# Where VectorE divides a unit of the memory attention: two steps behind its own maximum, instead of behind the next unit's

## The reference, cut to what matters

```python
def mem_attend(h, mk, mv, wq, wo):
    q = jnp.einsum('bsd,dhe->bshe', h, wq)
    s = jnp.einsum('bshe,bmhe->bhsm', q, mk.astype(q.dtype)).astype(jnp.float32) * MEM_SCALE
    pr = jax.nn.softmax(s, axis=-1).astype(q.dtype)
    o = jnp.einsum('bhsm,bmhe->bshe', pr, mv.astype(q.dtype))
    return jnp.einsum('bshe,hed->bsd', o, wo)
```

## Time and profile before

| | |
|---|---|
| median of 3 runs | 2026.81 us (2025.74 to 2030.93) |
| profiled execution | 2026.47 us, span 2024.7 us |
| mean granted TensorE clock | 0.971 |
| busy, share of the span | TensorE 94%, VectorE 49%, ScalarE 35%, GpSimd 5% |

### The profile page before, as it was taken

How to read it: one execution, slowest core, us unless ns; L and a number is a source line. 1 busy time by engine, 2 the same in 40 slices (tenths; PEclk the granted TensorE clock), 3 DMA queues, 4 the chain that set the end, 5 groups by cost and what they waited for, 6 DMA issues and landing times.

```text
span 2024.7 us, 37487 instructions
## 1 busy us (share of the span) xinstructions
PE 1897.0 (94%) x16506; PEld 1733.1 (86%) x16506; DVE 986.5 (49%) x1695; ACT 713.9 (35%) x1272; POOL 94.2 (5%) x100
## 2 busy tenths in 40 slices
PE   6998997999889999999999799989987999999997
PEld 5975775898679999999999478759974999999997
DVE  6676455453335544443367754455432465353533
ACT  4443444552334222221344344353523342121212
POOL 2000000200001000000100000001000100000001
PEclk9998999999999999999999799979999999999998
DMA  5210001453012222222222000014610222222221
GB/s 210 72 39 1 4 2 43 151 167 115 32 46 80 91 88 84 94 84 94 84 74 73 8 3 3 4 54 140 203 44 20 79 79 93 85 85 94 87 91 55
DMA packets 38593, 149.51 MB, mean 74 GB/s; under 512 B 4384, under 2 KB 4544, under 8 KB 36768
## 3 DMA queue, kind: packets, MB, share of 16 engines
q1 hardware_dynamic: 36288, 131.05, 19.6%
q0 software_dynamic: 2144, 16.06, 2.1%
HBM read 139.68 MB, written 7.41 MB: 73 GB/s over the span
## 4 chain that ended last, share of the span: by engine, by line
PE 88%; DVE 7%; ACT 3%; issue 1%; POOL 0%; DMA 0%; DVEq 0%; ACTq 0%; SPq 0%; POOLq 0%
PE PS L514 77%; PE PS L634 8%; PE PS L848 1%; DVE stat L1660 1%; PE PS L942 1%; DVE mP L1669 1%; DVE wL L1351 1%; ACT hH L973 1%; ACT wH L973 1%; POOL sq L450 0%; ACT ell L973 0%; DVE stat L1661 0%; ACT aP L973 0%; ACT sq L973 0%; DMA xT<-x_in 0%
## 5 line engine op out<-in xcount | busy, mean ns | idle before, releaser
L514 PE MATMUL PS<-hH,wH 128*128 128x272 f32 x2272 | 487.9, 297 | 31.3 <-DVE hL L1360 24.2
L514 PE MATMUL PS<-hH,wL 128*128 128x272 f32 x2272 | 476.3, 291 | 0.0
L514 PE MATMUL PS<-hL,wH 128*128 128x272 f32 x2272 | 475.9, 291 | 0.0
L1351 DVE TENSOR_TENSOR wL<-ring,wH 128x1024 fp32r<-128x1024 f32 x238 | 300.9, 1266 | 223.0 <-ACT wH L973 222.6
L514 PEld LDWEIGHTS PS<-hH,wH 128*128 128x128 f32 x2272 | 360.7, 190 | 43.4 <-issue 19.1
L973 ACT ACTIVATE wH<-ring 128x1024 fp32r<-128x1024 f32 x238 | 249.6, 1050 | 334.8 <-PE PS L514 334.8
L514 PEld LDWEIGHTS PS<-hH,wL 128*128 128x128 f32 x2272 | 362.2, 191 | 0.0
L514 PEld LDWEIGHTS PS<-hL,wH 128*128 128x128 f32 x2272 | 360.0, 191 | 0.0
L514 PE MATMUL PS<-hidH,wL 128*128 128x272 f32 x1024 | 212.1, 289 | 0.0
L514 PE MATMUL PS<-hidH,wH 128*128 128x272 f32 x1024 | 211.8, 288 | 0.0
L514 PE MATMUL PS<-hidL,wH 128*128 128x272 f32 x1024 | 211.2, 288 | 0.0
(11 more groups left out here) (279 smaller groups left out, 2476.5 us busy)
## 6 DMA issues: line engine op xcount, KB each, us to landing
ring<-wall SPq DMA_DIRECT2D x238, 512.0 KB, 3.3
lw<-lw_in POOLq DMA_DIRECT2D x2, 2240.0 KB, 9.8
xT<-x_in SPq DMA_DIRECT2D x4, 544.0 KB, 6.7
y_out<-hT SPq DMA_DIRECT2D x8, 272.0 KB, 2.1
mem<-mem_in POOLq DMA_DIRECT2D x2, 1024.0 KB, 5.2
mks<-mks_in POOLq DMA_DIRECT2D x2, 1024.0 KB, 10.1
mvs<-mvs_in POOLq DMA_DIRECT2D x2, 1024.0 KB, 13.4
memk_out<-mkp POOLq DMA_DIRECT2D x2, 1024.0 KB, 6.2
```

The lines of the kernel that those rows point to most:

```text
L514: return e.matmul(out, lhsT=a, rhs=b, start=start, stop=stop)
L1351: tt(wL[:, n % SPLIT], ring[:, n % RING], plain(wH[:, n % SPLIT]), ALU.subtract).then_inc(w_lo, 1)
```

## The change

VectorE's program walks the same list. It still takes the maximum at the score's step. The normalise of a unit no longer stands at the step of its turn but two steps behind its own score, from a table `DIVIDES`. So for all 20 units of both layers VectorE's order becomes normalise of u, then maximum of u + 1. TensorE's and ScalarE's programs are the same.

```diff
 MEM_STEPS += [("turn", len(MUNITS) - 1)] + [("weigh", 4 * MHEADS - 4 + _i) for _i in range(4)]
+
+DIVIDES = {_i + 2: _n for _i, (_kind, _n) in enumerate(MEM_STEPS) if _kind == "score"}
...
                 def attention_mem():
-                    for kind, n in MEM_STEPS:
-                        m = 128 if MUNITS[n][1] < 4 else DEC
+                    for i, (kind, n) in enumerate(MEM_STEPS):
                         if kind == "score":
-                            maximum(n, "m", m, MEM, MEM_SCALE, 4 + n % 2)
-                        elif kind == "turn":
-                            normalise(n, "m", mP, m, MEM)
+                            maximum(n, "m", 128 if MUNITS[n][1] < 4 else DEC, MEM, MEM_SCALE, 4 + n % 2)
+                        if i in DIVIDES:
+                            u = DIVIDES[i]
+                            normalise(u, "m", mP, 128 if MUNITS[u][1] < 4 else DEC, MEM)
                         yield
```

## The result

The changed kernel takes 1998.3 us (median of four runs, 1992.6 to 1999.9) against 2026.9 before, a ratio of 0.985 (95% interval 0.983 to 0.986). The forecast was 1994.3 us, a ratio of 0.984. The profiled execution took 1992.6 us with a span of 1990.8, 33.9 us less than before's span; worked out had been 32.5. It was the fastest of the four: its mean granted clock was 0.970, that of the others 0.964 to 0.967.

The account below looks back on a forecast made before the run. TensorE bounds the kernel, waiting for VectorE's divisions queued behind later maxima. Dense part 11.1 plus tail 5.2 give 16.3 us a layer, 32.5 for two, off the profiled 2026.47: 1994.0, as median 1994.3 us; range 1989 to 2004.

Parts of the forecast that it names:

- The bound: Where memory queries are projected, TensorE waits 32.0 us for the divided tile mP, held in VectorE's queue behind a later maximum.
- The dense part: While the query projection still runs, all waits of units 0 to 12 go: 11.06 us a layer.
- the walk: Step-by-step timing of the new order through the engines by the old trace's durations; 16.3 us a layer saved.
- The cover: Dense part: TensorE's other work hides the divisions, by over 0.8 us behind a query tile's evacuation, 0.3 at a head's end.
- The copy behind the next exponential at a head's end: ScalarE's copy of the turned unit may delay the weighing 0 to 0.3 us, two times a layer; taken as 0.
- The tail: Turns 13 to 19, without dense work beside them, fall from 20.1 to 14.9 us: 5.2 us a layer saved.
- What was to be seen: If right: mP wait falls from 32.0 to 6 to 10 us, all in the tails; a layer's stretch from 91.3 to 75.
- One sign of being wrong: A tail from the last dense step to the weighing of more than 16 us would speak against the forecast.
- Rival 1: Tail gains nothing, since ScalarE's copy may end last there; only units 0 to 13 count, 2001.8 us; chance 0.17.
- rival 3: No change: another wait, for the scores' banks or output copies, ends at the same time; 2026.8 us; chance 0.03.
- rival 4: Slower: VectorE waiting for ScalarE's exponential makes weight-tile splits late; 2030.9 us; chance 0.02.
- Rival 2: TensorE's clock: layer 1's weighing stays at full level, 1992.9 us, or layer 0's falls too, 1995.7; chance 0.08.

Follow-up runs that it names:

- both halves of the order: Two kernels, each giving only some units the change's order, the others as before: units 0 to 13 alone 2002.5 us, units 14 to 19 alone 2015.2 us.
- the pads: Changed kernel plus about 0.8 us idle VectorE work between exponential and reciprocal: units 0 to 12 in one kernel, 14 to 19 in another; 1999.6 and 2004.0 us.
- one-step order: Changed kernel with all divisions one step behind their own maximum instead of two; 1994.2 us (0.983).
- early rounding: ScalarE rounds oT's first three tiles right behind turn 19's copy, added to the kernel with ScalarE's early copy and a bank per last weighing; 1984.4 us (0.978).

## Why the prediction held, point by point

- The bound: TensorE, and its wait for VectorE's division. Shown by the totals and by both halves of the order, which take away their own waits and nothing else.
- The dense part, worked out at 11.1 us a layer: measured 11.5. All 13 waits went, as said. The transposes of the eleven full blocks are 0.06 us cheaper each without a wait, 0.66 us, which the walk had not counted. Those of the two stream units, 4 and 9, are not cheaper and start 0.34 instead of 0.25 us behind the last dense pair, so their waits were worth 0.09 us less than the walk took. 11.06 + 0.66 - 0.18 is 11.5.
- The cover: over 0.8 us for most, 0.3 at a head's end, by the walk. The pads show 0.7 at the end of head 0 and that 0.92 us more in front of every division costs 1.4 of 12 us. The walk was right in kind and too careful in size.
- The copy behind the next exponential at a head's end, 0 to 0.3 us: no wait in the dense part.
- The tail, worked out at 5.2 us: measured 4.7. The step that was off is "score 15 at 0.28": it must wait for the last query tile's evacuation, which VectorE starts 0.2 us behind the last dense step and takes 0.72 for, so it starts at 0.98. The walk had this evacuation in VectorE's row and forgot that TensorE waits for it. Before, unit 13's late turn had hidden it. It moved weighing 8 from 2.9 to 3.5, and the end from 14.9 to 15.4. That turns 16, 18 and 19 end the chains was right, as the pads show.
- What was to be seen: 6 to 10 us left of the wait for mP. There are 3.8 in both layers together, in the tails alone as said. The 6 to 10 did not fit the walk itself, whose waits before turns 14, 16, 18 and 19 (0.3, 0.5, 0.5 and 1.4) make 5.6 in both layers; turn 14's did not come, since score 15 was late. For mPT TensorE waits 3.0 us in both layers (2.4 before), for mq 1.2. One sign of being wrong did show, a tail of more than 16 us. It is 17.1 us in four of the eight layers profiled of the changed kernel and of its one-step order; 1.7 of these are the clock's, by one weighing, and not the order's.
- Rival 1 (2001.8) fell by experiment, rival 3 (no change) by the result, rival 4 by the one-step order and the pads. Rival 2, the clock, is real: in layer 1 of the change's first profile the long weighing ran at full speed, in other runs it or its like did not. That full speed gave the profile nothing, since the clock was then down for longer in the output projection: from the weighing's start to the first output tile's evacuation both kernels' layer 1 takes 17.84 us (1559.60 to 1577.44, 1525.00 to 1542.84). The Trainium skill ("TensorE: Matmul & The Clock Gate", What's actually happening) says that the same work can meet the clock differently from run to run, and this case's runs agree: in the changed kernel's layer 0 the same four matmuls took 1.98, 3.56 and 3.50 us in three profiled executions. Between the changed kernel's fastest and slowest execution lie 11 us, more than any unknown of the order.

So the number 1994.3 was right by its parts, 32.4 us for 32.5; that two misses of 0.4 and 0.5 us a layer had opposite signs was luck. The first median is 4.0 us above the forecast, and three of its four executions had a lower clock than the profiled one, by 0.003 to 0.006, which at 1.1 us for each 0.001 would make 3 to 7 us; the later medians, 1995.1 and 1995.7, are 0.8 and 1.4 above it.

## What to carry to other kernels

In a queue that runs strictly in order, look at what stands in front of an instruction that another engine waits for, not at how long it takes: here 0.5 us of work was late by 2.2 to 5.1 us in all units but the last, because the maximum of a later unit was queued first. Put the work of the older unit first, and walk the new order through all engines by the durations of the old trace; then ask of each instruction that now comes earlier what the old wait had hidden in front of it, as the evacuation here. The leftover waits of the new order (ScalarE's copy behind an exponential, one output bank for four products) were the next gains: 1984.4 us with them and the early rounding, beside 1995.7 for the change.

## What the runs showed of the hardware that was not expected

TensorE's granted clock fell behind gaps of under 2 us. In the changed kernel the four weighings behind the tail have gaps of 0.78, 0.38 and 0.78 us between them, and 1.68 us for hL follow. At the output projection's start the clock fell to 0.50, the lower level of 1.2 GHz. Within the projection's first 2 us it was at 0.50 in all twenty layers of the ten profiles in which the four weighings share one bank, before's among them. In the four layers of the two kernels with a bank for each of the last weighings it stayed at 1.00 there, although one of the two still has a wait of 1.80 us for hL. Which of the gaps brings the fall is not shown.

In the tails it fell in some executions and not in others, 1.5 to 1.7 us each time, with the old order in the tail and with the new one. Why one execution has it and the next has not stays open.
